# A 72-matmul opening rearranged, 24 bias-line instructions moved to the start, distance strips loaded in two halves

## What is computed

```python
mod = c @ w_ada[l] + b_ada[l]
shift, scale, gate = jnp.split(mod, 3, axis=-1)
h = rmsnorm(x, norm_g[l]) * (1.0 + scale[:, None]) + shift[:, None]
proj = h @ w_in[l]
...
bucket = t5_bucket(jnp.clip(dist, 0, n_back) * dil)
bias = jnp.transpose(bias_g[bucket].astype(jnp.float32), (2, 0, 1))
logits = jnp.einsum('znqhd,znkhd->znhqk', qb, kb).astype(jnp.float32) * (HEAD_DIM ** -0.5)
logits = jnp.where(mask[None, :, None], logits + bias[None, None], -jnp.inf)
```

## Time and profile before

| what | PE | DVE | ACT | POOL |
|---|---|---|---|---|
| busy, share of the span | 97% | 66% | 43% | 8% |
| share of the chain that ended last | 84% | 7% | 3% | 0% |

### The profile page before, as it was taken

The page is one execution under the profiler, slowest core; times in us unless marked ns, Lnnn a source line. Parts: engine busy times, 40 slices in busy tenths (PEclk is TensorE's granted clock), DMA queues, the critical chain, the costliest instruction groups (busy, mean ns, idle before and its releaser), DMA issues.

```text
span 1338.4 us, 24359 instructions
## 1 busy us (share of the span) xinstructions
PE 1292.9 (97%) x10441; PEld 1205.1 (90%) x10441; DVE 883.2 (66%) x1357; ACT 579.2 (43%) x892; POOL 102.9 (8%) x153
## 2 busy tenths in 40 slices
PE   5899999999999999999999999999999899899997
PEld 4799998899988788899998898998999899899997
DVE  3567755557544466467677687676778886767566
ACT  4434445543665544526422313213155664445431
POOL 0111100000001111000000011111100120000000
PEclk9899999999989999999999999999999999999999
DMA  9897886445244544032444356575434202555550
GB/s 349 307 332 233 264 241 181 142 146 161 93 128 161 187 153 163 33 121 101 148 150 158 115 173 202 172 236 190 127 127 158 64 1 64 170 191 191 183 180 33
DMA packets 163881, 218.40 MB, mean 163 GB/s; under 512 B 6030, under 2 KB 141589, under 8 KB 163638
## 3 DMA queue, kind: packets, MB, share of 16 engines
q1 hardware_dynamic: 140196, 148.11, 33.7%
q0 software_dynamic: 22880, 67.42, 16.0%
q10 hardware_dynamic: 698, 1.32, 0.3%
HBM read 215.70 MB, written 1.12 MB: 162 GB/s over the span
## 4 chain that ended last, share of the span: by engine, by line
PE 84%; DVE 7%; DMA 4%; ACT 3%; issue 2%; POOL 0%; SPq 0%; DVEq 0%; ACTq 0%
PE bank L1322 30%; PE bank L694 11%; PE bank L713 10%; PE bank L746 7%; PE bank L729 4%; DMA strip_b<-distance_parts 2%; PE bank L1399 2%; PE bank L1226 2%; PE bank L887 2%; PE bank L805 2%; PE bank L1414 1%; PE bank L1300 1%; DVE wlo L2079 1%; DMA graw_b<-in_w_mod 1%; PE bank L998 1%
## 5 line engine op out<-in xcount | busy, mean ns | idle before, releaser
L2079 DVE TENSOR_TENSOR wlo<-raw,whi 128x2048 fp32r<-128x2048 f32 x131 | 297.4, 2275 | 93.5 <-ACT whi L1493 93.2
L1493 ACT ACTIVATE whi<-raw 128x2048 fp32r<-128x2048 f32 x131 | 247.9, 1898 | 194.7 <-PE bank L1322 130.9
L1322 PE MATMUL bank<-whi,m_hi 128*128 128x256 f32 x576 | 160.4, 278 | 1.2 <-DVE m_lo L2677 0.8
L1322 PE MATMUL bank<-whi,m_lo 128*128 128x256 f32 x576 | 159.7, 277 | 0.0
L1322 PE MATMUL bank<-wlo,m_hi 128*128 128x256 f32 x576 | 159.7, 277 | 0.0
L1322 PE MATMUL bank<-a_hi,whi 128*128 128x256 f32 (+1 forms) x448 | 148.5, 332 | 0.0
L1322 PE MATMUL bank<-a_lo,whi 128*128 128x256 f32 (+1 forms) x448 | 148.1, 331 | 0.0
L1322 PE MATMUL bank<-a_hi,wlo 128*128 128x256 f32 (+1 forms) x448 | 148.0, 330 | 0.0
L1322 PEld LDWEIGHTS bank<-whi,m_hi 128*128 128x128 f32 x576 | 108.5, 188 | 1.9 <-DVE m_lo L2677 1.2
L1322 PEld LDWEIGHTS bank<-whi,m_lo 128*128 128x128 f32 x576 | 108.3, 188 | 0.0
L1322 PEld LDWEIGHTS bank<-wlo,m_hi 128*128 128x128 f32 x576 | 108.1, 188 | 0.1
(11 more groups left out here) (439 smaller groups left out, 3335.3 us busy)
## 6 DMA issues: line engine op xcount, KB each, us to landing
raw<-in_mlp_w SPq DMA_DIRECT2D x64, 1024.0 KB, 5.2
raw<-in_w_in SPq DMA_DIRECT2D x32, 1024.0 KB, 7.2
graw_b<-in_w_mod POOLq DMA_DIRECT2D x64, 512.0 KB, 4.9
raw<-in_ev_w_in SPq DMA_DIRECT2D x12, 1024.0 KB, 5.1
pre<-in_w_ada SPq DMA_DIRECT2D x16, 512.0 KB, 9.8
graw_a<-in_w_mod POOLq DMA_DIRECT2D x16, 512.0 KB, 7.1
Y<-in_w_mod POOLq DMA_DIRECT2D x16, 512.0 KB, 4.2
raw<-in_od_w_qkv SPq DMA_DIRECT2D x6, 1024.0 KB, 4.8
```

The lines of the kernel that those rows point to most:

```text
L1322: mm = nc.tensor.matmul(o, x, y, start=(k == 0 and i == 0), stop=(k == KT - 1 and i == 2))
L1493: nc.scalar.activation(split_pair(u, kt * cols)[0], landing(u, kt * cols), ACT.Copy).then_inc(hi_done, 1)
L2079: nc.vector.tensor_tensor(split_pair(u, n)[1], landing(u, n), bf(whi[u % HI], n), ALU.subtract).then_inc(lo_done, 1)
```

## The change

1. On ACT the loads of `hot` and `relb` go to the head of its queue, in front of the eleven small loads of vectors; a root of a constant follows them.
2. On PE the three bias lines move from behind unit 0 to between quarters 1 and 2. Their banks are now 0, 1 and 2, so the sixteen transposes wait until DVE has taken them (`line_done`). On DVE their copies stand ahead of the reciprocal; on POOL the write of `line` stands ahead of everything else.
3. On PE the first halves of units 0 to 2 are interleaved with quarters 8 to 15. Two k of unit 2 stand behind the last turn.
4. On DVE the sums of quarter 37 move to unit 20, and those of quarter 38 in front of the split of unit 24.
5. On POOL each strip is loaded in two transfers of 128 columns (384 KB): the halves with columns 128 to 255 ("near", semaphore `strip_near`) of both heads first, then the other two. `logits` at qt = 0 waits for the near halves, at qt = 1 for the other ones.

```diff
-        LINE_BANK = [bank[b] for b in (6, 4, 5)]
+        LINE_BANK = [bank[b] for b in (0, 1, 2)]
...
+            pool.wait_ge(line_done, 3)
+            pool.dma_start(parts.rearrange("h (v g w) -> h v g w", v=2, g=GROUPS), line[:, :, :, :]).then_inc(line_out, 16)
             pool.wait_ge(gemv_done, 13)
             for q in range(PRE_Q, PRE_Q + GSA):
                 load_q(q)
             load_q(PRE_Q + GSA)
-            pool.wait_ge(line_done, 3)
-            pool.dma_start(parts.rearrange("h (v g w) -> h v g w", v=2, g=GROUPS), line[:, :, :, :]).then_inc(line_out, 16)
...
+            for h2 in range(HEADS // 2):
+                for e in range(2):
+                    if h2:
+                        pool.wait_ge(at_s, 4 * h2 - 1 + e)
+                    elif e:
+                        pool.wait_ge(sum_step, sums_to(Q_B - 2))
+                    strip_part(2 * h2 + e, True)
+                for e in range(2):
+                    strip_part(2 * h2 + e, False)
...
             pe.wait_ge(cvec_done, 1)
-            for q in range(3):
+            for q in range(2):
                 gemv(q)
+            pe.wait_ge(load_w, 32)
+            for g in range(GROUPS):
+                distance_line(g)
+            gemv(2)
...
             gemv(3)
+            pe.wait_ge(line_done, GROUPS)
             pe.wait_ge(x_scaled, 1)
...
-            for u in range(EARLY):
-                unit_part(u, range(4))
-            for q in range(8, PRE_Q):
-                gemv(q)
-                if q == 13:
-                    gemv_turn(2)
+            unit_part(0, range(4))
+            gemv(8)
+            gemv(9)
+            unit_part(1, range(4))
+            gemv(10)
+            gemv(11)
+            unit_part(2, range(1))
+            gemv(12)
+            gemv(13)
+            gemv_turn(2)
+            gemv(14)
+            gemv(15)
+            unit_part(2, range(1, 2))
             gemv_turn(3)
+            unit_part(2, range(2, 4))
...
-                    pe.wait_ge(strip_full[e], 16 * (h2 + 1))
+                    pe.wait_ge((strip_full if qt else strip_near)[e], 16 * (h2 + 1))
...
+            act.dma_start(hot[:, :, :], cst[0:BUCKETS + 1, at["hot"][0]:at["hot"][0] + GROUPS * 384]
+                          .rearrange("p (g w) -> p g w", g=GROUPS)).then_inc(load_w, 16)
+            act.wait_ge(filled, FILLS)
+            act.dma_start(relb[0:BUCKETS, :], a["rel_bias"]).then_inc(load_w, 16)
+            nc.scalar.activation(stat[:, 61:62], stat[:, 40:41], ACT.Sqrt)
...
+                if u == 21:
+                    weighted_sums(PRE_Q + 22)
                 if u + LEAD > EARLY:
                     split_lo(u + LEAD)
                 b = before[u]
-                if u < 22 and u % 4 < 3:
+                if u < 21 and u % 4 < 3:
                     weighted_sums(PRE_Q + u)
-                if u == 21:
-                    weighted_sums(PRE_Q + 22)
+                if u == 20:
+                    weighted_sums(PRE_Q + 21)
```

More of the change, by code:

```diff
@@ L465, in build @@
         line_mm, line_done, line_out, strip_full = sem("line_mm"), sem("line_done"), sem("line_out"), [sem("strip_full0"), sem("strip_full1")]
+        strip_near = [sem("strip_near0"), sem("strip_near1")]
         sq_sum, root, x_scaled = sem("sq_sum"), sem("root"), sem("x_scaled")
@@ L631, in _, with strip_part @@
                     pool.dma_start(C[:, P + 6:keep], cst[:, P + 6:keep]).then_inc(load_k, 16)
[L632 to L640, removed]
+            def strip_part(h, near):
+                e = h % 2
+                pool.dma_start(strip[e][:, :, :, P:2 * P] if near else strip[e][:, :, :, 0:P],
+                               bass.AP(tensor=parts.tensor, offset=parts.offset + h * 2 * GROUPS * 384 + (P if near else 0),
+                                       ap=[[1, P], [GROUPS * 384, 2], [384, GROUPS], [1, P]]))\
+                    .then_inc((strip_near if near else strip_full)[e], 16)
+            for h2 in range(HEADS // 2):
[7 more added lines that the diff above has]
+                    strip_part(2 * h2 + e, False)
             pool.wait_ge(at_s, 2 * len(steps))
@@ L849, in quarters, with distance_line @@
                     gq[0] += 1
+            def distance_line(g):
+                nc.tensor.matmul(LINE_BANK[g][0:HEADS, 0:384], relb[:, g * HEADS:(g + 1) * HEADS], hot[:, g, :],
+                                 start=True, stop=True).then_inc(line_mm, 1)
             pe.wait_ge(cvec_done, 1)
-            for q in range(3):
+            for q in range(2):
                 gemv(q)
+            pe.wait_ge(load_w, 32)
+            for g in range(GROUPS):
+                distance_line(g)
+            gemv(2)
             pe.wait_ge(load_v, 16 * 11)
@@ L870, in _ @@
             gemv_turn(1)
-            def distance_line(g):
-                nc.tensor.matmul(LINE_BANK[g][0:HEADS, 0:384], relb[:, g * HEADS:(g + 1) * HEADS], hot[:, g, :],
-                                 start=True, stop=True).then_inc(line_mm, 1)
             def unit_part(u, ks):
@@ L901, in _ @@
                     unit_part(u, range(4, KT))
-                    if u == 0:
-                        pe.wait_ge(load_w, 32)
-                        pe.wait_ge(filled, FILLS)
-                        pe.wait_ge(mod_done, 4)
-                        for g in range(GROUPS):
-                            distance_line(g)
                 elif (u >= 4 and (u - 4) % 6 in (4, 5) and u < 22) or u >= 22:
@@ L1507, in _ @@
                 act.dma_start(brow[r0:r0 + rows, :], v).then_inc(load_v, 16)
-            act.dma_start(hot[:, :, :], cst[0:BUCKETS + 1, at["hot"][0]:at["hot"][0] + GROUPS * 384]
-                          .rearrange("p (g w) -> p g w", g=GROUPS)).then_inc(load_w, 16)
-            act.wait_ge(filled, FILLS)
-            act.dma_start(relb[0:BUCKETS, :], a["rel_bias"]).then_inc(load_w, 16)
             act.wait_ge(load_x, 16)
@@ L2097, in _ @@
             nc.vector.tensor_copy(cvec[:, 0, :], bank[6][:, 0:8]).then_inc(cvec_done, 1)
+            for g in range(GROUPS):
+                dve.wait_ge(line_mm, g + 1)
+                link(nc.vector.tensor_copy(line[:, 0, g, :], LINE_BANK[g][0:HEADS, 0:384]))
+                nc.vector.tensor_tensor(line[:, 1, g, :], LINE_BANK[g][0:HEADS, 0:384], line[:, 0, g, :].bitcast(f32),
+                                        ALU.subtract).then_inc(line_done, 1)
             dve.wait_ge(root, 1)
@@ L2136, in _ @@
             split_lo(EARLY)
-            for g in range(GROUPS):
-                dve.wait_ge(line_mm, g + 1)
-                link(nc.vector.tensor_copy(line[:, 0, g, :], LINE_BANK[g][0:HEADS, 0:384]))
-                nc.vector.tensor_tensor(line[:, 1, g, :], LINE_BANK[g][0:HEADS, 0:384], line[:, 0, g, :].bitcast(f32),
-                                        ALU.subtract).then_inc(line_done, 1)
             steps_of_sums = [0]
```

## The result

The changed kernel took 1331.13 us, median of 15 runs (1327.37 to 1333.86), beside 1338.66 us for the kernel before in 15 runs of the same comparison (1335.56 to 1345.13). The ratio is 0.9937 with a 95% interval of 0.9927 to 0.9947: 8.4 us less, between 7.1 and 9.8. This ratio is of the means, 1330.86 and 1339.28; the medians lie 7.5 us apart. Forecast were 1330 us and a change within 1%. The size fits too; that every term fits is another matter, and the rest of this text is about that.

What follows compares the result with a forecast made beforehand. PE was taken as the bound, with DMA engines filling the first 44 us. Terms of 6.4 us net before the attention and 3.5 for strips sum to 9.9, giving 1330 us, within 3 us at 0.58, with 1324 to 1336 as the range.

Steps and rivals of the forecast that it cites:

- Start until unit 0's first half: Opening up to unit 0: an earlier root gains nothing, since PE already waits for quarter 7's data; 0 us.
- Bias lines: Three line matmuls moved from behind unit 0 into PE's wait for quarter 2, hidden there: 2.4 us gained.
- the three line matmuls take 2.39 us and land in the 4.18 us: PE waits for quarter 2 from 8.43 to 12.61 us; the lines fit there, with 1.8 us to spare.
- Interleaved halves: Around the last turn: turn starts at 39.6 to 39.7 instead of 41.87, unit 0's second half at 42.6; 2.2 us gained.
- Clock: Unit 0's second half: less idle time keeps the clock at 1.00, 24 matmuls take 2.8 us, not 5.46; 2.6 us gained.
- Stall at the sums: Behind unit 3, sums of quarters 16 to 18: no stall or one of 2 us; 0.8 us taken as lost.
- Strips: Attention: moved sums end the first wait of 0.76 us, near halves both later ones; 3.5 us gained.
- Bytes decide: Strip loads: packet time follows bytes, so two near halves land after 6.2 us instead of 9.5; 2.7 us gained.
- Half only: Rival: clock falls again (2.6 less) or near halves land no earlier (2.7 less); 1332.9, with both 1335.6 us; chance 0.22.
- More than forecast: Rival: the half-clock stretch at 371.8 us may go too and unit 3 has no stall; 14.1 us gained, 1326.1; chance 0.12.
- Slower through the clock: Rival: interleaving thins PE's densest stretch, clock stays at 0.50 until unit 3; 2.2 us slower, 1342.4; chance 0.04.
- the reordering does nothing: Rival: quarter 15 lands 2.2 us later, so the last turn stays at 41.9; 1332.5 us; chance 0.04.

Runs made afterwards that it cites:

- the filler: Kernel before with eighteen matmuls of unread result added behind the last turn, nothing else moved: 1338.45 us median, 1.6 ± 0.6 us under before.
- the kernel without the early root: Changed kernel without the root of a constant at the start, timed twice: medians 1333.44 and 1331.34 us.
- whole strips: Changed kernel with each strip loaded whole in one transfer of 768 KB: 1330.74 us median, ratio 0.9936.
- whole strips and old sums: Changed kernel with strips loaded whole and the sums of quarters 37 and 38 at their old places: 1332.62 us median, ratio 0.9949.

## Why the prediction was right, point by point

**Start until unit 0's first half: 0.** Right as to what decides in most profiles: the transposes moved from 16.06 to 15.35, quarter 7's data came at 21.61 instead of 21.86, unit 0 began at 25.76 instead of 26.03. What it missed is that the other chain is only just hidden, and decides where the clock rises late.

**Bias lines: 2.4.** The step "the three line matmuls take 2.39 us and land in the 4.18 us" failed in its size: they take 4.01 there, at half rate, and leave nothing of the 1.8 us to spare. They were hidden all the same, since quarter 7 decides later. What they free at the old place is 2.1 us at full clock; 2.39 had 0.7 us of the half-clock stretch in it. Unit 3 shows 1.8, the time 0.8 ± 0.8. The copies' 0.6 us to spare were none either, by 0.4.

**Interleaved halves: 2.2.** Turn at 39.6 to 39.7 and second half at 42.6 were forecast; 39.5 and 42.21 came. PE's own 39.3 was the better of the two sums: quarter 15 was not waited for, as it landed at 37.66 and not at 38.4.

**Clock: 2.6.** The gap is the cause, shown by the filler and by the 14 profiles. Its size in the profile is right: 24 matmuls in 2.9 instead of 5.46. In time the term is mis-sized: the runs' mean clocks give 1.8 us, the gap's filling gave 1.6 ± 0.6. The prediction took the one profile that it had for every execution. Order and clock together gave 4.0 ± 0.7 alone, which is 2.2 + 1.8, and 1.8 ± 0.8 when taken back, where 4.8 were in the sum. Why taking back costs less than putting in gains is open.

The Trainium skill (TensorE: Matmul & The Clock Gate, Part 1: The HAM clock gate) says that the same kernel shows a different number of slow matmuls from run to run, at its start. The two profiles of the kernel without the early root agree: the clock's first record of 1.00 stands at 22.7 us in one and at 19.4 in the other, and the stretch behind it lasts 6.8 or 3.4 us.

**Stall at the sums: 0.8 lost.** None in the changed kernel: DVE's sum ended at 54.56 + 1.53 = 56.1 (forecast 55.7), and PE came at 56.59. The step was right in kind, for two variants have it, 0.47 us with whole strips and 0.42 with whole strips and old sums. Its premise shows as well: unit 4's data lands at 46.7 to 48.4 us in eight of the nine profiles with the new order, and at 43.7 to 44.2 in the five with the old one. That POOL's earlier loads are what delays it is the prediction's argument and was not tested. The margin is half a microsecond: the changed kernel's data lands at 46.72, that of the two variants at 47.51 and 48.38.

**Strips: 3.5.** Right in the trace and, at 2.7 to 2.8, within the error of the time. Near halves took 6.7 us, forecast 6.2; the prediction's estimate of 3.8 for them was far too low. "Bytes decide" is half right, and what was taken for its proof, the mean packet of two queues, mixes transfers of several kinds and sizes. The software queue in the 8 us in which the second pair's strips move, before (203 to 211 us) and after (195 to 203 us):

```profile
q0 software_dynamic: 1563, 1.57, 87.5%
```

```profile
q0 software_dynamic: 3123, 1.57, 109.0%
```

A packet of 1 KB takes 0.875 x 16 x 8.0 / 1563 = 72 ns, one of 512 bytes 1.09 x 16 x 8.0 / 3123 = 45 ns. It is 0.62 of the whole one's time, between 0.5 and 1. The Trainium skill (DMA: Bandwidth & Descriptors, Specifications) puts the smallest transfer at line rate at 512 bytes; here such a packet moves 11.5 bytes a nanosecond and a 1 KB packet 14.3, so in this case it is 0.8 of the rate.

**The sum.** 9.9 forecast; the profiled pair shows 11.3 up to the attention, with no stall and nothing of it lost, and 13.1 in all; the runs show 8.8 ± 0.6. By the parts alone: order 4.0, strips 2.7, root 0.4, lines 0.8 (by taking back), 7.9 in all. The clock (2.6 for 1.8), the lines (2.4 for 2.1 or less) and perhaps the strips (3.5 for 2.7) were taken too large, and only the stall of 0.8 us that did not come stood against them. That the sum is within 1.1 us is good fortune in part: the errors are small beside the whole, and one of them has the other sign.

**The rivals.** "Half only" did not happen as it was told: the stretch behind the last turn is in neither profile of the changed kernel, and near halves land earlier. That over many executions 0.7 of the clock's gain arrives is a part of its worry, at a price of 0.8 us and not 2.6. "More than forecast" is what the profiled execution shows, with the stretch of 371.8 us gone, but the runs' median doesn't, since that stretch comes and goes. "Slower through the clock" and "the reordering does nothing" are refuted by the row at 42.2 to 50.9 us and by the turn at 39.5.

## What to carry to other kernels

Time a stretch of matmuls by what the same matmuls take at both rates, and ask which rate holds at the new place: ahead of the clock's first record here it is the slow one. An idle gap of 2.3 us ahead of a dense stretch was worth closing, but for some 0.7 of the profile's gain: the mean granted clock of all timed runs, before and after, tells such a share where one profile can't. Where a part of a change makes PE earlier, look for the next transfer that PE meets: here one half of the change only kept its worth with the other.

## What the runs showed of the hardware that was not expected

- The granted clock reads 1.00 in the row at 8.5 to 12.5 us, while the line matmuls take 4.01 us against 2.10 at 45 us, and eight matmuls with a quarter 1.08 against 0.64. The clock's first record is of 17.7 to 22.7 us; ahead of it the column says nothing, and PE runs at half rate.
- That first record differs by 5 us between profiles. In the two of the kernel without the early root, at 22.7 and 19.4 us, unit 0 begins at 27.65 and 25.89, 1.8 us apart.
- Later than 360 us, the stretch in which every profile ends left out, a profile has none to four half-clock stretches, with PE busy for 81 to 100% of each, in kernels that are alike there. The one at 371.8 us alone made 2.9 us of the profiled pair's difference; the 15 runs of the changed kernel spread over 6.5 us.
- Packets of 512 bytes take 45 ns where those of 1 KB take 72, both in reads of `distance_parts` on POOL's queue.
